# Middle stage of a hybrid decoder layer: the turn of the modulations behind the sample's scores

## The reference

```
(s1, a1, g1, s2, a2, g2) = silu(c) @ w_ada + b_ada            # the modulations
h   = RMSNorm(x) * (1 + a1) + s1
[q | k | v | hc | B | C | ga | gb] = h @ w_in
A:  stick-breaking attention, beta = sigmoid(q.k/8 + b),
    A[t,s] = beta[t,s] * prod_{s<j<t} (1 - beta[t,j]); the sample also reads 2048 cached keys and values, by pages
B:  y = B * dwconv3_causal(C * hc)
mix = (sigmoid(ga) * (o_att @ w_att_out) + sigmoid(gb) * (y @ w_conv_out)) @ w_o
x   = x + g1 * mix
h2  = RMSNorm(x) * (1 + a2) + s2
x   = x + g2 * (relu(h2 @ w_mlp1)^2 @ w_mlp2)
```

## Time and profile before

| what | value |
|---|---|
| median of 3 runs | 1628.62 us (1628.6 to 1628.83) |
| profiled execution, its own time | 1628.18 us |
| its span | 1626.4 us |
| middle stage, ticks 0 to 47 in the trace | about 188 to 705 us |
| granted PE clock | 1.0 of full speed throughout |

### The profile page before, as it was taken

How to read it: one execution, slowest core, us unless ns; L and a number is a source line. 1 busy time by engine, 2 the same in 40 slices (tenths; PEclk the granted TensorE clock), 3 DMA queues, 4 the chain that set the end, 5 groups by cost and what they waited for, 6 DMA issues and landing times.

```text
span 1626.4 us, 31960 instructions
## 1 busy us (share of the span) xinstructions
PE 1613.1 (99%) x12386; PEld 1508.1 (93%) x12386; DVE 901.0 (55%) x1631; ACT 463.3 (28%) x813; POOL 607.1 (37%) x424
## 2 busy tenths in 40 slices
PE   8999999999999999999999999999999999999999
PEld 7998788888888888899999999999999999999999
DVE  5654354554553444325533799556666666666666
ACT  5444222222222222233222452222222222222220
POOL 0245143343344343412121127444444444444440
PEclk9999999999999999999999999999999999999999
DMA  9113446766656676434421111111111111111112
GB/s 382 53 44 99 159 149 216 234 208 235 206 186 222 215 249 230 153 132 174 171 106 40 40 39 53 40 53 53 36 44 53 53 53 53 52 53 53 53 40 107
DMA packets 72230, 194.76 MB, mean 120 GB/s; under 512 B 8049, under 2 KB 8562, under 8 KB 72082
## 3 DMA queue, kind: packets, MB, share of 16 engines
q1 hardware_dynamic: 67682, 178.62, 32.8%
q10 hardware_dynamic: 4400, 14.10, 2.2%
HBM read 174.26 MB, written 18.42 MB: 118 GB/s over the span
## 4 chain that ended last, share of the span: by engine, by line
PE 93%; DVE 2%; DMA 1%; ACT 1%; POOL 1%; issue 1%; SPq 0%; POOLq 0%; DVEq 0%; ACTq 0%
PE psum L827 79%; PE psum L964 2%; PE psum L987 2%; PE psum L1011 2%; PE psum L975 2%; PE psum L1036 2%; PE psum L859 1%; DMA ring<-in_cache_v 1%; POOL wl L728 1%; DVE h2L L1885 1%; DVE sc L1917 1%; DMA xt<-in_xT 0%; PE psum L888 0%; PE psum L995 0%; PE psum L876 0%
## 5 line engine op out<-in xcount | busy, mean ns | idle before, releaser
L810 POOL TENSOR_TENSOR wl<-raw,wh 128x512 fp32r<-128x512 f32 x148 | 212.6, 1441 | 317.2 <-ACT wh L1456 317.0
L827 PE MATMUL psum<-hH,wh 128*128 128x352 f32 x808 | 268.9, 333 | 0.1
L827 PE MATMUL psum<-hL,wh 128*128 128x352 f32 x808 | 260.0, 322 | 0.0
L827 PE MATMUL psum<-hH,wl 128*128 128x352 f32 x808 | 259.3, 321 | 0.0
L827 PE MATMUL psum<-hidH,wh 128*128 128x352 f32 x768 | 247.4, 322 | 0.0
L827 PE MATMUL psum<-hidH,wl 128*128 128x352 f32 x768 | 247.2, 322 | 0.0
L827 PE MATMUL psum<-hidL,wh 128*128 128x352 f32 x768 | 247.1, 322 | 0.0
L753 POOL TENSOR_TENSOR beta<-beta,kb 128x512 f32<-128x512 f32 (+3 forms) x96 | 122.5, 1296 | 248.7 <-DVE kb L1677 248.7
L728 POOL TENSOR_TENSOR wl<-raw,wh 128x1024 fp32r<-128x1024 f32 x49 | 119.6, 2440 | 231.4 <-ACT wh L1318 230.9
L827 PEld LDWEIGHTS psum<-hH,wh 128*128 128x128 f32 x808 | 151.5, 188 | 30.4 <-issue 29.3
L2004 DVE SCALAR_TENSOR_TENSOR act<-psum,mods,act 128x352 f32<-128x352 f32 x256 | 145.4, 580 | 50.5 <-PE psum L827 50.5
(11 more groups left out here) (255 smaller groups left out, 3254.9 us busy)
## 6 DMA issues: line engine op xcount, KB each, us to landing
raw<-in_weights SPq DMA_DIRECT2D x152, 512.0 KB, 3.7
ring<-in_cache_k SPq DMA_DIRECT2D x128, 256.0 KB, 3.9
ring<-in_cache_v SPq DMA_DIRECT2D x128, 256.0 KB, 3.7
pre<-in_weights SPq DMA_DIRECT2D x16, 512.0 KB, 16.6
gate_scratch<-gt ACTq DMA_DIRECT2D x14, 528.0 KB, 3.5
act<-gate_scratch SPq DMA_DIRECT2D x14, 528.0 KB, 4.6
xt<-in_xT SPq DMA_DIRECT2D x8, 528.0 KB, 6.9
act<-in_xT SPq DMA_DIRECT2D x8, 528.0 KB, 4.7
```

The source lines that it names most:

```text
L810: pool.tensor_tensor(xl, source_of(i), x.bitcast(F32), ALU.subtract).then_inc(S["split"], 1)
L827: mm = pe.matmul(out, x, y, start=n == 0, stop=n == end)
```

## The change

In PE's loop `sample_scores` moves ahead of `ada_turn` with its waits. In DVE's loop `history` moves ahead of `modulation`. Nothing is added or taken away.

```
@@ PE @@
                 if 0 < k <= NSTEP:
                     turn(k - 1)
+                if k in ITEM_AT:
+                    sample_scores(ITEM_AT[k], k)
                 if k in ADA_TURN_AT:
                     pe.wait_ge(S["beta_done"], min(2 * k + 2, 2 * NSTEP))
                     if k in TURN_AT:
                         pe.wait_ge(S["s_at"], TURN_AT[k] + 1)
                     ada_turn(ADA_TURN_AT[k], ada_ps)
-                if k in ITEM_AT:
-                    sample_scores(ITEM_AT[k], k)
                 if k in DENSE_B and k:
                     dense(DENSE_B[k], hH, hL)
@@ DVE @@
                 if 0 < k <= NSTEP:
                     turned(k - 1)
+                if k in HISTORY_AT:
+                    history(HISTORY_AT[k])
                 if k in ADA_TURN_AT:
                     modulation(ADA_TURN_AT[k], ada_ps[:, 0:9])
-                if k in HISTORY_AT:
-                    history(HISTORY_AT[k])
                 if k in ITEM_AT:
                     sample_scan(ITEM_AT[k])
```

## The result

The change makes the kernel slower: 1632.74 us (1632.40 to 1633.22, median of 12 runs) against 1628.72 us (1628.37 to 1629.54, 12 runs) of the kernel before. The ratio is 1.0024, with a 95% interval of 1.0016 to 1.0032. The forecast of 1630.4 had the sign right, but the change costs +4.0 where +1.8 was forecast, and its time lies 0.4 above the range. The profiled execution's own time is 1632.72, its span 1630.9. The granted clock is 1.0 throughout in both.

A forecast was written before the change was run, and what follows sets the result against it. PE was taken as the bound, busy 1613.1 of 1626.4 us. Terms +6.5 - 1.0 - 2.7 - 1.0 = +1.8 on 1628.18 gave 1630.0, or 1630.4 after 0.44 to the runs' median; range 1627.9 to 1632.3.

The forecast's parts named there:

- The sign: Whole kernel: the change makes it slower, by +1.8 us.
- the three kinds of tick: PE's middle stage: twelve ticks with second `dense` -2.7 us; eleven without +6.5 - 1.0; two of those give back 1.0.
- the removed wait: PE ahead of L995: scores cover DVE's copy, saving 2.7 us in nine ticks and 1.0 in ticks 10 and 21.
- the round trip through DVE: Eleven ticks without second `dense`: `ada` waits for DVE's read, 0.62 us after the turn; 0.59 more per tick, 6.5 us.
- scores to turn at 1.01: PE, start of scores to start of full-width turn: 1.01 us taken; at 0.90 the sum would be -0.7.
- the waits of L995 for DVE's copy: PE's turn of the modulations waiting for `s_at`: 3.7 us in eleven ticks by the loads' idle time, expected to go.
- DVE's part at nothing: DVE's `history` ahead of `modulation` in four ticks: costed at nothing, could add some 0.2 us where `ada` follows at once.
- Ticks 33 and 37: PE already waits there for cached values behind `ada`, so lateness is absorbed: 0.41 and 0.59, together 1.0 us given back.
- the slower rival: SP's loads fall behind because `ada` ends later: +3.4 us from one further late page, 1632.0; chance 13%.
- turn to what follows: PE from the turn's start to the next product: 0.62 us to `ada`, 0.14 to dense.
- the change of width costs nothing: Rival for PE's step from scores to turn: 0.90 us, sum -0.7, 1627.9 us; chance 10%.
- L995's idle time on the loads: PE's weight loads for the turn of the modulations: idle time ahead falls from 3.7 us to near 0.

The follow-up runs named there:

- experiments 1 and 2: The changed PE order only in the twelve ticks with a second `dense`: 1627.06 us, ratio 0.9990; only in the eleven without: 1634.60 us, ratio 1.0036.
- experiment 5: Changed kernel, but in the eleven ticks without a second `dense` the turn writes a free dense bank, so `ada` need not wait for DVE: 1628.34 us.
- experiment 8: Kernel before with only DVE's `history` moved ahead of `modulation`, PE's order unchanged: 1628.65 us against 1628.77.
- experiment 6: Changed kernel with the turn as four 32-column products in the 23 ticks with scores ahead of it, full width elsewhere: 1628.66 us, ratio 1.0001.
- experiment 3: Changed kernel with the turn as four 32-column products in the array's column groups in all ticks: 1630.50 us, ratio 1.0011 against the kernel before.
- experiments 7 and 9: Kernel before with the turn ahead of the transposes, but behind the scores in three ticks (1626.13 us) or, in column groups, in twelve (1623.63 us).

## Why the prediction was wrong

**Right.** The sign; the three kinds of tick (experiments 1 and 2); that the removed wait is bought with the round trip through DVE (experiment 5); scores to turn at 1.01, the value chosen between 0.90 and 1.01; the waits of L995 for DVE's copy, gone; DVE's part at nothing (experiment 8). Ticks 33 and 37 gave back about 0.9 of the 1.0 forecast, but with a row that differs by 1 us between profiles that is luck as well. The loads did not fall behind, the slower rival's mechanism; the time passed its +3.3 by another road.

**Wrong: the step "turn to what follows", in both terms that use it.** I took 0.62 for turn to `ada` from tick 46 and 0.14 for turn to dense from tick 3. In both of those ticks the turn stands behind full-width transposes, and its load is 0.107 ahead. The change puts it behind column groups, and I had priced that only up to the turn's start, in the 1.01. It goes on inside the turn: its load is not ahead, its second pass comes 0.1 later, and so do DVE's begin or the dense product behind it. With the measured steps, 0.14 more in eleven ticks and 0.06 more in three of these is 1.7, and 0.105 more in twelve ticks is 1.3. A part of the 1.7, 0.05 per tick, is that `ada` starts 0.10 and not 0.05 after DVE's end.

A smaller error went the other way. The eleven turns that waited before had their second pass 0.07 late, and the idle time of the loads does not count that. Start to start, from transposes to scores, the removed waits are 2.9 and 1.1 and not 2.7 and 1.0. With all these the sum is 1.8 + 1.7 + 1.3 - 0.3 = +4.5, against +4.7 measured in the 23 ticks (6.41 - 1.67).

The rival "the change of width costs nothing" fell: scores to turn is 1.01 and not 0.90, and experiment 6, which takes that change away ahead of the turn, gets back as much as the whole change lost. About 2.0 us of it belong to the 3.0 that the forecast missed here. The bounds were too narrow at this place. I looked for bounds of the step into the turn and of DVE's begin, and gave the turn itself one length. It had never been seen behind the neighbour that it was getting, but the rows of before had a longer one: in tick 8 the pair is 0.36 long, and 283.98 - 283.69 = 0.29 passes to the scores, where tick 40 takes 633.47 - 633.24 = 0.23. That would have given about 0.06 of the 0.10.

**Also wrong:** that L995's idle time on the loads would go to nearly nothing. It is 4.4 us (22 times some 0.2), the same change of width seen from the load's side. A total in a group's row can stay while its cause is exchanged.

**Open:** why the load is not ahead where the width changes, beyond that it is so in either direction (experiments 3 and 6); why `ada` starts 0.10 after DVE's end in these ticks; and how much of experiments 7 and 9 the cached pages took.

## What to carry to other kernels

Before a small piece is moved off a wait, look at what covered its own round trip: here the scores hid DVE's read of the turn, and moving them away cost more (experiment 5: 4.4 us of the run's time) than the wait it removed (some 4.0). Take the duration of a moved step from a row in which the step has the same neighbours, the width of the array ahead of it above all, and if there is no such row, bound the step's inside and not only its start: a row in which the same step had no load ahead for another reason, here a wait, gives a first size. In this kernel a small full-width product was cheapest among full-width ones, or cut into its neighbours' column groups; which of the two was chosen place by place, and that was worth 5 us over the kernel before.

## What the runs showed of the hardware

- A full-width fp32 product of 9 columns is recorded as two passes. In all 64 turns of the traces before and after, the second pass starts 0.134 to 0.139 us after the start of the first pass's load. It follows the first pass by 0.030 to 0.041 where that load began 0.09 to 0.11 ahead of its matmul (behind full-width products), by 0.103 where the turn had waited for a semaphore and the load began 0.03 ahead, and by 0.133 behind products of 32 array columns, where load and matmul begin together.
- The same product as eight passes of 32 columns has its first load some 0.11 ahead behind the scores' column groups, in 22 of 23 places, and its passes start some 7 ns apart (experiment 6). Behind full-width transposes its loads are not ahead, and it starts 0.20 behind the last of them, where the full-width product starts 0.11 behind (experiment 3, nine ticks).
- The round trip PE, DVE, PE for a 128x9 result cost 0.62 to 0.82 us from the full-width turn's start to the next product (ticks 46 of before and after, eleven ticks of after), of which DVE's own operation is 0.22 to 0.29.
